# Moving the transposes of the normed residual from TensorE to the DMA queue in a two-layer hybrid decoder trunk

## What is computed

```python
for l in range(2):
    h = rms_norm(x, attn_pre_g[l])                 # "pre"
    u = h @ w_in[l]                                # 1024 -> 2560, ten blocks of 256
    y = concat(conv_mixer(u[:2G]), retention(...), moba_attention(...), pool_mixer(...))
    x = x + rms_norm(y @ w_out[l], attn_post_g[l]) # "post"
    h = rms_norm(x, ffn_pre_g[l])                  # "fpre"
    f = silu(h @ w_gate[l]) * (h @ w_up[l])        # 1024 -> 2816, twice
    x = x + rms_norm(f @ w_down[l], ffn_post_g[l]) # "fpost"
```

## Time and profile before

| | us |
|---|---|
| median of 3 runs | 1108.68 (1108.66 to 1112.82) |
| the profiled execution | 1109.05 |
| its span | 1107.2 |
| TensorE busy in it | 1079.1 |
| VectorE busy | 620.5 |
| ScalarE busy | 410.3 |

### The profile page before, as it was taken

One profiled execution on the slowest core, in us unless ns is written; L12 is line 12 of the kernel. 1 busy time (PEld: TensorE's weight loads), 2 busy tenths in 40 slices (PEclk: granted clock), 3 DMA queues, 4 the chain that ended last, 5 costly groups with the idle time before them and its releaser, 6 DMA issues.

```text
span 1107.2 us, 16624 instructions
## 1 busy us (share of the span) xinstructions
PE 1079.1 (97%) x6640; PEld 656.5 (59%) x6640; DVE 620.5 (56%) x1418; ACT 410.3 (37%) x810; POOL 5.1 (0%) x18
## 2 busy tenths in 40 slices
PE   5999999999999999999999999999999999999997
PEld 4888785596444444444478878747844444444443
DVE  5898998884324324312568989889624324322014
ACT  4454635454323323212234463455523323322001
POOL 1000000000000000000000000000000000000000
PEclk9999999999999999999999999999999999999999
DMA  7442403155234233233003341034533333232001
GB/s 272 132 131 77 154 1 115 39 177 164 80 113 149 80 114 112 95 99 114 1 1 115 115 135 57 1 114 135 176 110 110 101 113 111 81 113 76 1 20 57
DMA packets 58172, 109.64 MB, mean 99 GB/s; under 512 B 7024, under 2 KB 7280, under 8 KB 57968
## 3 DMA queue, kind: packets, MB, share of 16 engines
q1 hardware_dynamic: 58096, 108.58, 31.1%
HBM read 106.46 MB, written 2.10 MB: 98 GB/s over the span
## 4 chain that ended last, share of the span: by engine, by line
PE 88%; DVE 6%; DMA 4%; issue 1%; ACT 1%; SPq 0%; ACTq 0%; DVEq 0%
PE ps L493 82%; DMA raw<-weights_dram 3%; PE ps L497 3%; DVE ring L1134 2%; DVE E L1255 2%; PE ps L696 1%; PE ps L680 1%; DMA gbc<-gains_dram 1%; DVE E L1207 0%; ACT ring L758 0%; DVE small L1437 0%; DVE hT L1215 0%; ACT gbc L758 0%; DVE U L1358 0%; PE ps L657 0%
## 5 line engine op out<-in xcount | busy, mean ns | idle before, releaser
L493 PE MATMUL ps<-hT,ring 128*128 128x512 f16 (+1 forms) x3264 | 549.0, 330 | 2.8 <-DVE hT L1215 2.7
L493 PEld LDWEIGHTS ps<-hT,ring 128*128 128x128 f16 x3264 | 320.4, 98 | 226.6 <-issue 3.1
L493 PE MATMUL ps<-ring,U 128*128 128x512 f16 x1440 | 313.4, 379 | 0.0
L1134 DVE SCALAR_TENSOR_TENSOR ring<-raw,ring 128x512 f16<-128x512 f32 x376 | 236.8, 685 | 97.5 <-ACT ring L758 96.7
L758 ACT ACTIVATE ring<-raw 128x512 f16<-128x512 f32 x376 | 212.9, 622 | 140.3 <-PE ps L493 81.2
L493 PEld LDWEIGHTS ps<-ring,U 128*128 128x128 f16 x1440 | 140.8, 98 | 167.1 <-issue 0.3
L1458 DVE SCALAR_TENSOR_TENSOR R<-ps,R 128x512 f32<-128x512 f32 (+1 forms) x52 | 31.7, 609 | 255.4 <-ACT R L933 255.0
L493 PE MATMUL ps<-ring,hT 128*128 128x256 f16 x1152 | 134.3, 273 | 0.0
L933 ACT ACTIVATE R<-ps 128x512 f32<-128x512 f32 (+1 forms) x52 | 27.5, 530 | 275.4 <-PE ps L493 275.4
L493 PEld LDWEIGHTS ps<-ring,hT 128*128 128x128 f16 x1152 | 112.2, 98 | 14.2 <-issue 1.1
L1255 DVE SCALAR_TENSOR_TENSOR E<-E,par 128x256 f32<-128x256 f32 x240 | 101.7, 477 | 0.2
(11 more groups left out here) (104 smaller groups left out, 475.7 us busy)
## 6 DMA issues: line engine op xcount, KB each, us to landing
raw<-weights_dram SPq DMA_DIRECT2D x376, 256.0 KB, 3.4
gbc<-gains_dram SPq DMA_DIRECT2D x8, 512.0 KB, 6.1
xs<-x_dram SPq DMA_DIRECT2D x4, 512.0 KB, 5.3
out_dram<-xs SPq DMA_DIRECT2D x8, 256.0 KB, 2.0
cst<-consts_dram SPq DMA_DIRECT2D x1, 1296.0 KB, 8.2
bd<-pool_w_dram SPq DMA_DIRECT2D x8, 16.0 KB, 5.6
par<-params_dram SPq DMA_DIRECT2D x1, 76.0 KB, 6.0
cst<-consts_dram SPq DMA_DIRECT2D x1, 64.0 KB, 5.8
```

The source lines that it names most:

```text
L493: ins = mm(dst, st, mv_, start=first and i == 0, stop=last and i == 2, **kw)
L1134: V.scalar_tensor_tensor(out=ring[:, slot % RING, 1, raw_part(part)], in0=raw[:, n % NRAW, :], scalar=W_SCALE, in1=ring[:, slot % RING, 0, ...
```

## The change

Only "pre" of layer 0 still goes through `h_T`. For the other three norms `norm_x` writes the normed tile in fp32, token-major, to the tile's two banks of PSUM; `h_hi_of` and `h_lo_of` write the fp16 halves token-major to SBUF (`xh`, `xl`: the two `xn` buffers for fpre, the buffer `R` for pre), and SP turns each half with one DMA with `transpose=True` into `hT`, 128 x 1024 elements each. SP does so behind the last part of the weight slot that `HT_AFTER` names, after waiting for both halves; slots count through both layers, so 51 is slot 4 of layer 1. TensorE waits for `hT_in` of the tiles of the unit. A buffer is free when the DMAs of the tile two before it have landed (`xh_free`). The banks of PSUM are given back when the low half is written (`norm_done`). Several waits on `hT_ps` go. The table `AT` and the orders of ScalarE and VectorE are written anew for both layers: the small products of the mixers move by up to some twenty ticks. The diff, cut to its core:

```diff
@@ -118,31 +118,44 @@
 AT = [
     {
...
-        ("fpre_T", 0): 371, ("fpre_T", 1): 376, ("fpre_T", 2): 433, ("fpre_T", 3): 436, ("pre_T", 0): 948,
-        ("pre_T", 1): 970,
...
+HT_AFTER = {
+    ("fpre", 0, 0): 18,
+    ("fpre", 0, 1): 18,
+    ("fpre", 0, 2): 20,
+    ("fpre", 0, 3): 20,
+    ("pre", 1, 0): 51,
+    ("pre", 1, 1): 51,
+    ("pre", 1, 2): 52,
+    ("pre", 1, 3): 52,
+    ("fpre", 1, 0): 65,
+    ("fpre", 1, 1): 65,
+    ("fpre", 1, 2): 67,
+    ("fpre", 1, 3): 67,
+}
...
         m_at = 6 * HALF
         xn = [E[:, m_at:m_at + DM], E[:, 4672 - 4 - DM:4672 - 4]]
+        xsplit = {"fpre": [x_.bitcast(F16) for x_ in xn], "pre": [R[:, DM * i:DM * (i + 1)].bitcast(F16) for i in range(2)]}
...
+        hT_in = [sem(f"hT_in{t}") for t in range(NT)]
...
+        def by_pe(kind, l):
+            return kind == "pre" and l == 0
+        def xh(kind, t):
+            return xsplit[kind][t % 2][:, 0:DM]
+        def xl(kind, t):
+            return xsplit[kind][t % 2][:, DM:2 * DM]
+        def hT_no(kind, l):
+            return 32 * (2 * l + (kind == "fpre"))
         def raw_part(i):
             return slice(RAW * i, RAW * (i + 1))
+        def xh_free(eng, kind, l, t):
+            if t >= 2:
+                eng.wait_ge(hT_in[t - 2], hT_no(kind, l))
+            elif kind == "pre":
+                eng.wait_ge(f_lo, len(HIDDEN) * l)
+            elif t == 1:
+                eng.wait_ge(convT_ps, hs(l, 1))
+                eng.wait_ge(mY_ps, hs(l, 1))
...
+            def h_T_load(kind, l, t):
+                sp.wait_ge(h_hi, xno(kind, l, t) + 1)
+                sp.wait_ge(h_lo, xno(kind, l, t) + 1)
+                for half_, src in enumerate((xh(kind, t), xl(kind, t))):
+                    sp.dma_start(hT[:, half_, :, tok(t)], src, transpose=True).then_inc(hT_in[t], 16)
...
+                for (kind, i, t), slot in HT_AFTER.items():
+                    if n == PARTS * (slot + 1) - 1:
+                        h_T_load(kind, i, t)
...
+            def norm_done(kind, l, t):
+                if kind == "post":
+                    return h_lo, xno("fpre", l, t) + 1
+                if l + 1 < L:
+                    return h_lo, xno("pre", l + 1, t) + 1
+                return x_upd, yno(kind, l, t) + 1
...
-                if pre:
+                if pre and by_pe(pre, l):
                     pe.wait_ge(h_lo, xno(pre, l, tiles[-1]) + 1)
+                elif pre:
+                    for tile in tiles:
+                        pe.wait_ge(hT_in[tile], hT_no(pre, l))
...
-                            take(b, x_upd, yno(kind, l, t) + 1)
+                            take(b, *norm_done(kind, l, t))
...
-                    if at == AT[l]["pre_T", t]: h_T("pre", l, t)
+                    if by_pe("pre", l) and at == AT[l]["pre_T", t]: h_T("pre", l, t)
...
-                for t in TILES:
-                    if at == AT[l]["fpre_T", t]: h_T("fpre", l, t)
-                if l + 1 < L:
-                    for t in (0, 1):
-                        if at == AT[l]["pre_T", t]: h_T("pre", l + 1, t)
...
-                act.wait_ge(hT_ps, xno(kind, l, t) + 1)
-                copy(hT[:, 0, :, tok(t)], pair(t).rearrange("p (k t) -> p k t", k=KT),
-                     A_SCALE / RN).then_inc(h_hi, 1)
+                if by_pe(kind, l):
+                    act.wait_ge(hT_ps, xno(kind, l, t) + 1)
+                    copy(hT[:, 0, :, tok(t)], pair(t).rearrange("p (k t) -> p k t", k=KT),
+                         A_SCALE / RN).then_inc(h_hi, 1)
+                    return
+                act.wait_ge(xn_sb, xno(kind, l, t) + 1)
+                xh_free(act, kind, l, t)
+                copy(xh(kind, t), pair(t), A_SCALE / RN).then_inc(h_hi, 1)
...
-                if n > 1:
+                if by_pe(kind, l) and t > 1:
                     dve.wait_ge(hT_ps, n - 1)
-                if kind == "fpre" and t == 1:
-                    dve.wait_ge(convT_ps, hs(l, 1))
-                    dve.wait_ge(mY_ps, hs(l, 1))
-                V.scalar_tensor_tensor(out=xn[t % 2], in0=xs[:, t, :], scalar=r, in1=gbc[:, 1, :], op0=ALU.mult,
+                dst = xn[t % 2] if by_pe(kind, l) else pair(t)
+                V.scalar_tensor_tensor(out=dst, in0=xs[:, t, :], scalar=r, in1=gbc[:, 1, :], op0=ALU.mult,
...
-                V.scalar_tensor_tensor(out=hT[:, 1, :, tok(t)], in0=pair(t).rearrange("p (k t) -> p k t", k=KT),
-                                       scalar=A_SCALE / RN, in1=hT[:, 0, :, tok(t)], op0=ALU.mult,
+                if by_pe(kind, l):
+                    V.scalar_tensor_tensor(out=hT[:, 1, :, tok(t)], in0=pair(t).rearrange("p (k t) -> p k t", k=KT),
+                                           scalar=A_SCALE / RN, in1=hT[:, 0, :, tok(t)], op0=ALU.mult,
+                                           op1=ALU.subtract).then_inc(h_lo, 1)
+                    return
+                xh_free(dve, kind, l, t)
+                V.scalar_tensor_tensor(out=xl(kind, t), in0=pair(t), scalar=A_SCALE / RN, in1=xh(kind, t), op0=ALU.mult,
                                        op1=ALU.subtract).then_inc(h_lo, 1)
...
+                if l and s == 0:
+                    for t in TILES:
+                        dve.wait_ge(hT_in[t], hT_no("pre", l))
...
+                norm_x("pre", l, 2)
+                z = l * SLOTS
                 norm_y("fpost", l - 1, 3)
-                zero(l)
-                norm_x("pre", l, 2)
                 norm_x("pre", l, 3)
+                h_lo_of("pre", l, 2)
                 glu(l, 0)
-                h_lo_of("pre", l, 2)
-                conv(l, 0, 1)
+                split_lo(z + 4)
                 h_lo_of("pre", l, 3)
-                conv(l, 0, 4)
-                z = l * SLOTS
...
                 norm_y("post", l, 1)
                 norm_x("fpre", l, 0)
                 norm_x("fpre", l, 1)
                 h_lo_of("fpre", l, 0)
-                split_lo(z + 17)
                 h_lo_of("fpre", l, 1)
                 norm_y("post", l, 2)
+                split_lo(z + 18)
                 norm_y("post", l, 3)
-                split_lo(z + 18)
                 norm_x("fpre", l, 2)
+                norm_x("fpre", l, 3)
+                h_lo_of("fpre", l, 2)
+                h_lo_of("fpre", l, 3)
                 split_lo(z + 19)
                 hidden_steps(l, 0, 1)
-                norm_x("fpre", l, 3)
                 split_lo(z + 20)
-                h_lo_of("fpre", l, 2)
-                h_lo_of("fpre", l, 3)
                 split_lo(z + 21)
                 hidden_steps(l, 1, len(HIDDEN))
+                hidden_lo(l, *HIDDEN[-1])
                 split_lo(*(z + DN0 + c + RING for c in range(N_DN - DN_TAIL)))
-                hidden_lo(l, *HIDDEN[-1])
                 norm_y("fpost", l, 0)
                 norm_x("pre", l + 1, 0)
                 norm_y("fpost", l, 1)

...
```

More of the change, by code:

```diff
@@ L120 @@
     {
[L121 to L125, removed]
@@ L131 @@
-        ("pre_T", 1): 970,
-    },
-    {
[L134 to L143, removed]
-    },
-]
+        ("pre_T", 2): 54, ("pre_T", 3): 58, ("moba_T", 0): 115, ("moba_T", 1): 129, ("moba_stage", 0): 136,
@@ new lines @@
+        ("moba_stage", 1): 154, ("moba_T", 2): 158, ("moba_stage", 2): 162, ("moba_stage", 3): 169,
+        ("moba_stage", 4): 175, ("moba_stage", 5): 175, ("moba_Y", 0): 178, ("moba_T", 3): 188,
+        ("conv_T", 0): 188, ("moba_stage", 6): 196, ("moba_stage", 7): 213, ("ret_T", 0): 215,
+        ("conv_Y", 0): 217, ("ret_S", 0): 218, ("ret_O", 0): 223, ("ret_T", 1): 223, ("moba_stage", 8): 223,
+        ("ret_S", 1): 224, ("ret_O", 1): 228, ("moba_stage", 9): 257, ("moba_stage", 10): 275,
@@ new lines @@
+        ("ret_T", 2): 277, ("moba_stage", 11): 281, ("moba_Y", 1): 282, ("pool_Y", 0): 282, ("ret_S", 2): 290,
+        ("ret_T", 3): 295, ("ret_Y", 0): 296, ("ret_O", 2): 301, ("ret_S", 3): 304, ("ret_O", 3): 313,
+        ("conv_T", 1): 313, ("conv_Y", 1): 324, ("pool_Y", 1): 337, ("ret_Y", 1): 349,
+    },
+    {
+        ("moba_T", 0): 94, ("moba_T", 1): 105, ("moba_stage", 0): 118, ("moba_stage", 1): 139,
+        ("moba_T", 2): 148, ("moba_stage", 2): 153, ("moba_stage", 3): 158, ("moba_stage", 4): 163,
+        ("moba_stage", 5): 164, ("moba_T", 3): 168, ("moba_Y", 0): 168, ("conv_T", 0): 177,
+        ("moba_stage", 6): 195, ("moba_stage", 7): 203, ("ret_T", 0): 208, ("conv_Y", 0): 209,
+        ("ret_S", 0): 210, ("ret_O", 0): 216, ("ret_T", 1): 217, ("moba_stage", 8): 219, ("ret_S", 1): 223,
+        ("ret_O", 1): 227, ("moba_stage", 9): 242, ("moba_stage", 10): 276, ("moba_stage", 11): 282,
+        ("ret_T", 2): 284, ("pool_Y", 0): 284, ("moba_Y", 1): 286, ("ret_S", 2): 292, ("ret_T", 3): 295,
+        ("ret_Y", 0): 298, ("ret_O", 2): 301, ("ret_S", 3): 302, ("ret_O", 3): 308, ("conv_T", 1): 313,
+        ("conv_Y", 1): 325, ("pool_Y", 1): 341, ("ret_Y", 1): 350,
+    },
+]
@@ L1033, in _ @@
[L1033 removed]
+                split_hi(z + 16)
                 conv_scale(l, 1)
                 conv_affine(l, 1)
```

(7 more changed lines are left out.)

168 lines of the change are left out of this document (82 added, 86 removed).

## The result

| | before | after |
|---|---|---|
| median, same chip, us | 1111.17 (9 runs) | 1116.48 (9 runs, 1113.45 to 1122.51) |
| ratio | | 1.0052, 95% interval 1.0036 to 1.0068 |
| profiled execution, us | 1109.05 | 1115.67 |
| its span, us | 1107.2 | 1113.3 |

What follows compares the result with a forecast made beforehand. TensorE, busy 97% of the span, was taken as the bound. Removing 10.4 us and adding 3.0 us of waits gave net -7.4 from 1109.05: 1101.7, or 1101.3 against the median, stated as 1101.5; 8-in-10 range 1097 to 1145.

Steps and rivals of the forecast that it cites:

- What is removed: Twelve of sixteen h_T calls leave TensorE, in fpre of both layers and pre of layer 1: 12 x 0.87 = 10.4 us.
- d: Time by which each transposing DMA delays the next on SP's queue; taken as 1.0 us.
- the forecast's sign: In the profile after, each transposing DMA's issue on SP would take under 1 us.
- Rival 1: The wait replaces the removed work: d between 1.2 and 2.4, net -5.6 to +5.2 us, time the same; chance 0.22.
- Rival 2: Slower: transposing DMAs move at the pace of their 256-byte runs, d above 2.4, 1120 us at 3.0; chance 0.35.
- D: Pre tiles 2 and 3, tick 64 of layer 1: TensorE waits 3d - 3.0 us for transposes.
- A: Fpre tiles 0 and 1, first FFN unit: wait 3d - 3.1 us, about a microsecond roomier in layer 1.
- B: Fpre tiles 2 and 3, tick 448: wait 3d - 1.5 us, less what A has already waited.
- C: Pre tiles 0 and 1, tick 0 of layer 1: transposes hidden up to d of about 3.
- the same holds for the reordered small products of both layers: Reordering the mixers' small products was booked at 0, with 1 to 2 us either way in the range.
- the granted clock still 1.00: Sign expected in the profile after: the granted clock stays at 1.00.
- The covers: Weight parts of slots 19, 21, 51 and 53 behind SP's wait for the halves stay covered unless d nears 3.

## Why the prediction was wrong, point by point

**What is removed: right.** 10.4 us was forecast, 9.6 in the trace and 9.4 by the medians (1110.7 - 1101.3) were measured.

**d: the term that was mis-sized.** "I take d = 1.0, between the two rates of whole weight parts" took the rates of weights for those of transposes. From the first issue to the last of a unit, d = (238.2 - 233.4) / 3 = 1.6 for tick 448 of layer 0, 1.7 for the two late units of layer 1 (578.5 to 583.7, 773.9 to 779.1), and 1.4 for the early ones (210.5 to 214.6). Two things ran at about that pace. SP was held 1.24 to 1.44 us for each, where the forecast's sign was under 1, and 2.0 to 2.5 for one of four in the dense stretches. And the DMA engines were full at 194 GB/s, which is 1.35 us for 256 KB. The runs separate the two only in part: with one DMA for a tile SP was free 1.2 us sooner in a unit and the landing 0.5 us or nothing sooner, which speaks for the engines. So the bound from the 0.33 us of a plain issue and the 0.66 us of the densest stretch were no bounds of this instruction. Rival 1's sentence, that a transposing issue may need more commands, fits SP's 1.3 us. Rival 2's pace of the 256-byte runs fits the engines, at a much lower price. The page has 25344 more packets of under 512 B than that of before (32368 against 7024), 1056 for each DMA, as rival 2 counted them. With them the packets of q1 took 34.0% of 16 x 1113.3 us in place of 31.1% of 16 x 1107.2, which is an estimate of 22 ns for each new packet, not 95, and 64 of them are 1.4 us. The 95 ns were a mean over packets that mostly carry 2 KB. Of the Trainium skill's rules, the one in "Advanced Engine Details and Errata", section X-Bar Transpose (TRN2), that such DMAs are as fast as regular ones, agrees with the landing (3.3 us against 3.4 to 3.5 for a weight part) and not with the pace: 256 KB every 1.4 to 1.7 us are 150 to 190 GB/s, where it gives 350 to 400. The 1309 ns in "VectorE: DVE Perf Modes", section The three transpose paths, does not hold block by block here: a DMA of eight blocks was issued in 1.3 us.

**The waits: the mechanism and the places right, and the sizes follow from d.** With d = 1.7, D = 3d - 3.0 gives 2.1, measured 2.3. With 1.6, A and B of layer 0 together 3d - 1.5 = 3.3, measured 0.8 + 2.6 = 3.4; layer 1 with 1.7 3.6, measured 0.7 + 2.9. C was hidden, as said, but with 2.3 us to spare where the forecast had 5.3: tile 1's DMAs went out at 556.8. SP's first issue for B was forecast 16.3 us behind the wanted start of the FFN, and was 16.2 behind it. With d = 1.6 the sum of the prediction is 9d - 6.0 = 8.4, net -2.0, 1107 us, rival 1's "same". Measured waits: 9.4. So d takes away 5.4 of the 7.4 us that were forecast, and the sign comes from what follows.

**Three things the sum didn't have.** First, "the same holds for the reordered small products of both layers", booked at 0 with 1 to 2 us either way: layer 0 lost 3.1 us at tick 64. It could have been read off: the diff puts `split_lo(z + 4)`, four times 0.62, ahead of `h_lo_of` of tile 3, for which TensorE waits, and layer 0 has no DMA that would need it. The run without DMAs, which keeps the wait, and the one with the old mixing, which has none, show it to be the order. Second, "the granted clock still 1.00": twice in layer 1 it fell to its lower level behind a wait, and the next 16 ticks took 1.66 us longer each time, 3.3 in all. Third, 0.6 us at tick 464, where PSUM is freed late. 8.4 + 3.5 + 3.3 + 0.6 = 15.8 of the 16.6 us that were added. The time lies within the range given, but by luck: the range reached there for the sake of rival 2 with d above 2.4, and d was 1.4 to 1.7.

**The covers.** "Behind SP's wait for the halves stand the weight parts [...] so they are covered unless d nears 3" was right for after, and wrong as a rule: one slot earlier, the same parts were late enough to stall TensorE through the order of VectorE.

## What to carry to other kernels

Transposing DMAs in a row do not follow each other at the rate of plain loads of the same bytes: here each 256 KB took 1.4 to 1.7 us of the queue, and four times the issue of a weight part. Work out how many stand in a row ahead of the first consumer, and take that as the latency. When a step moves to a queue, its place in the queue and the order of every engine that shares data with what stands behind it have to be chosen together: here the change cost 5 us net in one order and gained 5 to 6 in another. A unit that keeps the old way (here pre of layer 0) should keep the old order too.
